# The 32-row sample tile of every projection in plain fp32, its 512 columns in four strips of 32 PSUM rows

## The chip, the cores and the metric

The kernel runs on one core of a Trainium2 chip, as one launch. Its time is the device time of one execution in microseconds (us). All rows below come from one profiled execution of it.

## The reference

The program is one inference step of a two-layer decoder for 512 prompt rows and 32 sample rows (8 sequences of 4 new tokens), all in fp32. Layer A mixes tokens with a gated MLP, layer B with differential attention over shared keys and values; after each mixer comes a mixture of 16 experts, two for each token. `x` stands for prompt and sample rows together, 544 of them.

```python
# layer A
z = gelu(x @ w_in + b_in)                # 1024 -> 2048
u, v = split(z);  v = layer_norm(v)
x = layer_norm(ALPHA * x + (u * mix(v)) @ w_out)
x = layer_norm(ALPHA * x + moe(x))       # router, top 2 of 16 experts
# layer B
k, v, q = x @ w_k, x @ w_v, x @ w_q      # 1024 -> 1024 each
x = layer_norm(ALPHA * x + heads_norm(attention(q, k, v, cache)) @ w_o)
x = layer_norm(ALPHA * x + moe(x))
```

## The kernel before

**Tiles.** The 544 rows are five tiles: four of 128 prompt rows and one of the 32 sample rows (`TILES`, `ROWS`, the sample tile is `t == TILES - 1`). A projection's weights come in blocks of 512 output columns: 4 for `w_in`, 2 for `w_out`, 6 for K, V and Q, 2 for `w_o`, so 14 blocks. A block is two chunks, for the two halves of the 1024 input rows (`kh`); a chunk is 1 MB, four groups (`j`) of 128 input rows by 512 columns.

**The split product.** Every matrix is split in two: `wh` is the chunk rounded to fp32r (ScalarE, line 617), `wl` the rest (VectorE, line 868). The input rows are transposed on TensorE (`turn`, line 1467), ScalarE rounds them into `xTh` (line 632), and VectorE takes the rest into `xTl` (line 882). A product is then three matmuls of fp32r operands (`three`, lines 1422 to 1424), with the transposed rows stationary (128 or 32 columns of them) and 512 weight columns moving. For each of 8 groups of input rows, each of the five tiles costs these three matmuls.

**Order.** `project` runs a block half by half, all five tiles in each half; `project_by_tile` runs tile after tile, both halves at once, and is used for `w_out`, the first K block and `w_o`. A tile's result lies in one of six PSUM banks (`bank_for`); VectorE evicts it (lines 934, 977 and 1267) and gives the bank back with `proj_free`. The order on each engine is the order in which the code is written. In a `w_in` block VectorE splits two chunks first and evicts then; in the third block it computes the statistics of a layer norm in between (lines 889 to 899), in the fourth it ends that layer norm (line 914).

**Buffers.** Chunks land in six `raw` slots, asked for by SyncE's queue in a written order. A slot is asked for again when VectorE has split what is in it (`low["a"]`, `low["b"]`). The split chunks lie in three slots of `wh` and `wl`, which come free with `used` when TensorE is done with a half block.

**Around the projections.** After `w_out` and after `w_o` come a layer norm, tile by tile over all engines (`ln_tiles`), and the router (`route`): TensorE transposes a tile and multiplies it with the router's weights (lines 1538 and 1541), and VectorE works out from the logits which expert gets which row. Ahead of this, `moe_act` and `moe_dve` split the first two chunks of the first expert. Attention (lines 1657 to 1760) uses plain fp32 matmuls, the sample's value product among them (line 1720, 32 stationary and 128 moving columns, once for each head):

```python
for h in range(HEADS):
    mm = pe.matmul(ps[0:NSAMP, 6 + h // 4, h % 4 * P:(h % 4 + 1) * P], ptz[:, page, b2, h],
                   vals[:, page, h * P:(h + 1) * P], ...)
```

Of the kernel before, what the change touches and what calls it, by code (L numbers as in the profile page):

```python
# [123 lines left out]
def trunk(nc, a, outs):  # L124
    y_prompt, y_sample, k_prompt, v_prompt, k_sample, v_sample, state_v = outs
    with ExitStack() as ctx:
# [19 lines left out]
        xTh = place("xTh", [P, KT_D, NTOK], F32R)[0]  # L146
        xTl = place("xTl", [P, KT_D, NTOK], F32R)[0]
# [9 lines left out]
        rwh, rwl = rwhl[:, :, 0], rwhl[:, :, 1]  # L157
        rbias = place("rbias", [P, EXPERTS], F32)[0]
# [20 lines left out]
        xT0 = place("xT0", [P, KT_D, NTOK], F32, arena)[0]  # L179
        rw_raw = place("rw_raw", [P, KT_D, EXPERTS], F32, arena + 20480)[0]  # L180
# [16 lines left out]
        mxs, n = place("mxs", [P, 4, 2, 2], F32, n)  # L197
        o = [o01[:, 0], o01[:, 1], o23[:, 0], o23[:, 1], o4[:, 0]]
# [3 lines left out]
        Es, n = place("Es", [P, 288], F32, n)  # L202
        Ps, n = place("Ps", [P, 288], F32, n)
# [3 lines left out]
        assert n <= split_at  # L207
# [85 lines left out]

        def dram_tile(t, ap):
            return ap[t * P:t * P + ROWS[t]]
# [22 lines left out]
        def _(sp):  # L318
# [50 lines left out]
            def x_half(half):  # L369

                for dst, src in ((xT0[:, 4 * half:4 * half + 4, 0:SEQ], a["x_prompt_T"]),
                                 (xT0[:, 4 * half:4 * half + 4, SEQ:NTOK], a["x_sample_T"])):
# [17 lines left out]
            def after_a(slot):  # L390
# [4 lines left out]
                else:  # L395
                    sp.wait_ge(low["a"], low_a[c])
# [9 lines left out]
            for c in range(B_CHUNKS):  # L406
# [10 lines left out]
                else:  # L417
                    sp.wait_ge(low["b"], low_b[c - RAW_SLOTS])
# [12 lines left out]
            def after_b(slot):  # L431
# [3 lines left out]
                else:  # L435
                    sp.wait_ge(low["b"], low_b[c])
# [4 lines left out]
        def _(pool):  # L441
# [19 lines left out]
            pool.dma_start(rw_raw[:], a["router_w"].rearrange("(k p) e -> p k e", p=P)).then_inc(rw_in, 16)  # L461
# [146 lines left out]
        def _(act):  # L608
# [50 lines left out]
            for half in range(2):  # L659
                act.wait_ge(xT0_in[half], 32)  # L660
                act.activation(xTh[:, 4 * half:4 * half + 4], xT0[:, 4 * half:4 * half + 4], ACT.Copy).then_inc(x0_high, 1)
                split_a(half)
            act.wait_ge(rw_in, 16)
            act.activation(rwh, rw_raw[:], ACT.Copy).then_inc(rw_high, 1)
# [191 lines left out]
        def _(dve):  # L856
# [20 lines left out]
            def turn_low(n0, gain=1.0):  # L877
                for n in (n0, n0 + 1):
                    t, half = n % 10 // 2, n % 2
                    dve.wait_ge(tr_high, n + 1)  # L880
# [926 lines left out]
```

## Time and profile before

| what | value |
|---|---|
| three timed runs | 1462.28, 1470.77 and 1472.52 us, median 1470.77 |
| span of the profiled execution, first to last instruction | 1465.0 us |
| its mean granted clock of TensorE, as a share of 2.4 GHz | 0.912 |
| TensorE matmuls, busy | 1253.8 us (86%) |
| TensorE weight loads, busy | 963.9 us (66%) |
| VectorE, busy | 916.1 us (63%) |
| ScalarE, busy | 698.6 us (48%) |
| GpSimd, busy | 252.7 us (17%) |

No time beside the span is listed for the profiled execution itself; the span is 5.8 us under the median of the timed runs. PE is TensorE, PEld its weight loads, DVE VectorE, ACT ScalarE, POOL GpSimd, SP SyncE. L1422 is line 1422 of the kernel. Busy time of matmuls counts their durations, which overlap in a pipeline; the distance from one start to the next is what one costs.

### The profile page before, as it was taken

To read this page: it belongs to the slowest core of one execution; us is meant where nothing else is said; L and a number is where in the kernel's file an instruction comes from. 1 tells how busy PE (TensorE), PEld (TensorE's weight loads), DVE (VectorE), ACT (ScalarE), POOL (GpSimd) and SP (SyncE) were. 2 spreads that over 40 slices of the span, in tenths; PEclk is the share of its full clock that TensorE was granted. 3 is DMA by queue.
4 is the path that set the end of the run, shared out by engine and by line. 5 is a ranking of instruction groups with operands and counts; after the bars stand their busy time and mean duration, and the time that the engine had idled before them with its cause. 6 is when DMAs were issued, how large, how long until landed. Compare 5 with 4: busy or idle time off the path is not lost.

```text
span 1465.0 us, 16900 instructions
## 1 busy us (share of the span) xinstructions
PE 1253.8 (86%) x5888; PEld 963.9 (66%) x5888; DVE 916.1 (63%) x1112; ACT 698.6 (48%) x748; POOL 252.7 (17%) x261
## 2 busy tenths in 40 slices
PE   5989994599999996299999999989937999999930
PEld 4766764478888885277776666657736788888820
DVE  4256357498888885832321444464675988888836
ACT  4233223277777775222112544432224777777721
POOL 2021020241111121410000000000302411112314
PEclk9999995699999998599999999969858999999975
DMA  9302047269999996732230133213462899999842
GB/s 341 122 29 93 1 173 285 84 224 359 374 372 372 376 368 214 296 116 92 89 116 1 59 116 115 78 48 118 187 238 83 302 376 373 369 375 371 299 181 77
DMA packets 142529, 302.56 MB, mean 207 GB/s; under 512 B 11888, under 2 KB 12048, under 8 KB 142352
## 3 DMA queue, kind: packets, MB, share of 16 engines
q1 hardware_dynamic: 123024, 250.23, 47.9%
q0 software_dynamic: 19168, 51.31, 9.8%
q8 instruction: 30, 0.49, 0.1%
q10 hardware_dynamic: 288, 0.36, 0.1%
q14 instruction: 19, 0.16, 0.0%
HBM read 288.36 MB, written 30.28 MB: 217 GB/s over the span
## 4 chain that ended last, share of the span: by engine, by line
PE 78%; DVE 13%; DMA 3%; ACT 3%; issue 2%; POOLq 0%; POOL 0%; SPq 0%; DVEq 0%; ACTq 0%
PE ps L1422 20%; PE ps L1424 20%; PE ps L1423 20%; PE ps L1657 3%; DVE wl L868 2%; PE ps L1720 2%; PE ps L1705 2%; PE ps L1581 2%; DVE x L1225 2%; PE ps L1467 2%; ACT wh L617 2%; PE ps L1674 1%; PE ps L1691 1%; DMA xg<-x_rows,gcur 1%; DMA yl<-y_rows 1%
## 5 line engine op out<-in xcount | busy, mean ns | idle before, releaser
L868 DVE TENSOR_TENSOR wl<-raw,wh 128x2048 fp32r<-128x2048 f32 x210 | 481.0, 2314 | 221.3 <-ACT wh L617 217.4
L617 ACT ACTIVATE wh<-raw 128x2048 fp32r<-128x2048 f32 x210 | 398.4, 1915 | 202.0 <-PE ps L1424 138.0
L1422 PE MATMUL ps<-wh,xTh 128*128 128x512 f32 (+1 forms) x560 | 227.7, 407 | 22.8 <-DVE wl L868 14.8
L1424 PE MATMUL ps<-wh,xTl 128*128 128x512 f32 (+1 forms) x560 | 223.0, 398 | 0.0
L1423 PE MATMUL ps<-wl,xTh 128*128 128x512 f32 (+1 forms) x560 | 223.0, 398 | 0.0
L1422 PE MATMUL ps<-wh,xgTh 128*128 128x512 f32 x512 | 209.3, 409 | 6.7 <-DVE xgTl L1175 5.7
L1423 PE MATMUL ps<-wl,xgTh 128*128 128x512 f32 x512 | 203.9, 398 | 0.0
L1424 PE MATMUL ps<-wh,xgTl 128*128 128x512 f32 x512 | 203.5, 398 | 0.0
L1422 PEld LDWEIGHTS ps<-wh,xTh 128*128 128x128 f32 (+1 forms) x560 | 98.6, 176 | 58.9 <-issue 22.5
L1422 PEld LDWEIGHTS ps<-wh,xgTh 128*128 128x128 f32 x512 | 97.3, 190 | 36.2 <-DVE wl L868 8.3
L1424 PEld LDWEIGHTS ps<-wh,xTl 128*128 128x128 f32 (+1 forms) x560 | 98.0, 175 | 34.2
L1423 PEld LDWEIGHTS ps<-wl,xTh 128*128 128x128 f32 (+1 forms) x560 | 98.7, 176 | 31.9
L1422 PE MATMUL ps<-wh,hTh 128*128 128x512 f32 x256 | 106.0, 414 | 9.9 <-DVE hTl L1186 9.9
L1424 PEld LDWEIGHTS ps<-wh,xgTl 128*128 128x128 f32 x512 | 97.2, 190 | 24.2
L1423 PEld LDWEIGHTS ps<-wl,xgTh 128*128 128x128 f32 x512 | 97.5, 190 | 20.5
L1424 PE MATMUL ps<-wh,hTl 128*128 128x512 f32 x256 | 103.7, 405 | 0.0
L1423 PE MATMUL ps<-wl,hTh 128*128 128x512 f32 x256 | 103.2, 403 | 0.0
L1279 DVE TENSOR_REDUCE mxs<-ps 128x1 f32<-128x256 f32 (+3 forms) x64 | 31.4, 491 | 85.8 <-PE ps L1659 85.4
L517 POOL COPY gcur<-gidx 128x1 int32 (+1 forms) x34 | 18.3, 537 | 356.6 <-PE ps L1581 295.3
L458 POOL TENSOR_TENSOR x<-x,gb 128x1024 f32<-128x1024 f32 x16 | 45.8, 2864 | 157.1 <-ACT x L648 157.1
L703 ACT ACTIVATE xgTh<-ps 128x1024 fp32r<-128x1024 f32 x34 | 34.9, 1027 | 59.9 <-PE ps L1581 59.8
L1422 PEld LDWEIGHTS ps<-wh,hTh 128*128 128x128 f32 x256 | 49.6, 194 | 21.0 <-DVE wl L868 10.4
(258 smaller groups left out, 1641.1 us busy)
## 6 DMA issues: line engine op xcount, KB each, us to landing
raw<-in_moe_w_up SPq DMA_DIRECT2D x120, 1024.0 KB, 10.5
raw<-in_moe_w_down SPq DMA_DIRECT2D x62, 1024.0 KB, 11.7
raw<-in_a_w_in SPq DMA_DIRECT2D x8, 1024.0 KB, 16.7
ahead_up<-in_moe_w_up SPq DMA_DIRECT2D x8, 1024.0 KB, 8.7
yl<-y_rows POOLq DMA_DIRECT2D x8, 1024.0 KB, 8.4
raw<-in_cache_k SPq DMA_DIRECT2D x16, 512.0 KB, 3.8
raw<-in_cache_v SPq DMA_DIRECT2D x16, 512.0 KB, 4.9
raw<-in_a_w_out SPq DMA_DIRECT2D x4, 1024.0 KB, 5.1
```

The costliest lines, as they stand in the source:

```text
L458: pool.tensor_tensor(src[0:m, t], src[0:m, t], gb[0:m, 0:D] if call else x[0:m, 0], ALU.mult).then_inc(ln_gain, 1)
L617: act.activation(wh[:, slot], src, ACT.Copy).then_inc(high[key], 1)
L703: act.activation(xgTh[:], ps[:, 2:4].rearrange("p a (k m) -> p (a k) m", m=P), ACT.Copy).then_inc(s["xg_high"], 1)
L868: dve.tensor_tensor(wl[:, slot], src, wh[:, slot].bitcast(F32), ALU.subtract).then_inc(low[key], 1)
L1225: link(dve.scalar_tensor_tensor(out=x[0:m, t], in0=yl[0:m, t, k], scalar=gates[0:m, k, t:t + 1], in1=x[0:m, t], op0=ALU.mult, op1=ALU.add))
L1279: dve.tensor_reduce(mxs[:, 1, n % 2, part:part + 1], ps[:, part, 0:w], AX, ALU.max, negate=True).then_inc(at_max, 1)
L1422: pe.matmul(out, high_, w_high, start=start, stop=False)
L1423: pe.matmul(out, high_, w_low, start=False, stop=False)
L1424: return pe.matmul(out, low_, w_high, start=False, stop=stop)
L1467: mm = pe.transpose(ps[:, 6 + n % 2, j * P:j * P + m], src[0:m, k * P:(k + 1) * P], ident[0:m, 0:m])
L1581: mm = pe.transpose(ps[:, 2 + k // 4, k % 4 * P:(k % 4 + 1) * P], xg[:, k * P:(k + 1) * P], ident)
L1657: pe.matmul(ps[:, part, 0:w], QT[r, h, qt * P:(qt + 1) * P], KT[r, h, 0:w], start=True, stop=False, skip_group_check=True)
```

## The change

The sample tile leaves the split product. Its transposed rows lie in `xs` as plain fp32, and the weights are read unsplit from the `raw` slot. For each group of 128 input rows there are four matmuls in the place of three: each has the same 32 stationary columns and 128 of the 512 moving columns, and piece `c` writes PSUM rows `32c` to `32c + 31` of the tile's bank. The 128-row tiles stay as they were. The rest follows from that: VectorE evicts the tile in four pieces; ScalarE no longer copies the sample's transposed rows, VectorE does it alone; the sample's router product is plain fp32 too; and a `raw` slot is asked for again when TensorE has used it (`used`), no longer when VectorE has split it (`low`).

```diff
+        def strip(step, c):
+            return ps[32 * c:32 * c + NSAMP, step % PROJ_BANKS, 0:P]
+        def raw_of(key, s):
+            c = s + (s >= A_WS) if key == "a" else s if s < B_CACHE else s - B_CACHE + B_WO
+            return raw[:, c % RAW_SLOTS]
...
                 if c >= RAW_SLOTS:
-                    sp.wait_ge(low["a"], low_a[c - RAW_SLOTS])
+                    sp.wait_ge(used["a"], low_a[c - RAW_SLOTS])
...
                     t, half = n % 10 // 2, n % 2
+                    if t == TILES - 1:
+                        continue
                     act.wait_ge(tr_done, n + 1)
...
+                    if t == TILES - 1:
+                        dve.wait_ge(tr_done, n + 1)
+                        dve.tensor_scalar(xs[:, 4 * half:4 * half + 4],
+                                          ps[:, 6 + n % 2].rearrange("p (k m) -> p k m", k=4)[:, :, 0:NSAMP],
+                                          gain, None, ALU.mult).then_inc(tr_low, 1)
+                        continue
...
+                if t == TILES - 1:
+                    for c in range(4):
+                        w = x[0:m, t, cb * HALF + c * P:cb * HALF + (c + 1) * P]
+                        ins = dve.scalar_tensor_tensor(out=w, in0=w, scalar=ALPHA, in1=strip(m_step, c),
+                                                       op0=ALU.mult, op1=ALU.add)
+                    ins.then_inc(proj_free, 1)
+                    return
...
+            def sample_tile(key, s, kh, step):
+                for j in range(4):
+                    k = 4 * kh + j
+                    for c in range(4):
+                        mm = pe.matmul(strip(step, c), xs[:, k], raw_of(key, s)[:, j, c * P:(c + 1) * P],
+                                       start=(k == 0), stop=(k == KT_D - 1), skip_group_check=True)
+                return mm
...
-                        for j in range(4):
+                        if t == TILES - 1:
+                            mm = sample_tile(key, s, kh, m0 + t)
+                        for j in range(4 if t < TILES - 1 else 0):
```

On TensorE, in the first half of the first block, where the fourth 128-row tile ends and the sample tile begins, there stood before (`ps` is PSUM, the shape is that of the output; the three rows of 32x512 then come three times more):

```order
L1422 MATMUL ps<-wh,xTh 128x512
L1423 MATMUL ps<-wl,xTh 128x512
L1424 MATMUL ps<-wh,xTl 128x512
L1422 MATMUL ps<-wh,xTh 32x512
L1423 MATMUL ps<-wl,xTh 32x512
L1424 MATMUL ps<-wh,xTl 32x512
```

And at the same place now:

```order
L1458 MATMUL ps<-wh,xTh 128x512
L1459 MATMUL ps<-wl,xTh 128x512
L1460 MATMUL ps<-wh,xTl 128x512
L1472 MATMUL ps<-raw,xs 32x128 x16
L1458 MATMUL ps<-wh,xTh 128x512 [waits x0_low,low_a]
```

Twelve matmuls of 512 columns have become sixteen calls of 128 columns.

On ScalarE, after `w_out`, in the layer norm and router of layer A, up to the first expert's splits and the exponential of the router, there stood before:

```order
L632 ACTIVATE xTh<-ps 128x4x128 [waits tr_done] x2
L646 ACTIVATE lns<-lns 32x1 [waits ln_var]
L648 ACTIVATE x<-x,lns 32x1024 [waits ln_rs]
L632 ACTIVATE xTh<-ps 128x4x128 [waits tr_done] x4
L632 ACTIVATE xTh<-ps 128x4x32 [waits tr_done] x2
L617 ACTIVATE wh<-raw 128x2048 [waits raw_m0_0,used_a]
L617 ACTIVATE wh<-raw 128x2048 [waits raw_m0_1,used_a]
L699 ACT_TABLE_LOAD
```

And now:

```order
L644 ACTIVATE xTh<-ps 128x4x128 [waits tr_done] x2
L658 ACTIVATE lns<-lns 32x1 [waits ln_var]
L660 ACTIVATE x<-x,lns 32x1024 [waits ln_rs]
L644 ACTIVATE xTh<-ps 128x4x128 [waits tr_done] x4
L627 ACTIVATE wh<-raw 128x2048 [waits raw_m0_0,used_a]
L627 ACTIVATE wh<-raw 128x2048 [waits raw_m0_1,used_a]
L711 ACT_TABLE_LOAD
```

The two copies of the sample tile between the last full tile and the first expert's splits are gone.

On SyncE's queue, from the `w_in` chunks after the first six to the first expert's chunks, there stood before:

```order
L386 DMA raw<-in_a_w_in 128x4x512 [waits low_a] x2
L386 DMA raw<-in_w_s_T 128x1024 [waits low_a]
L386 DMA raw<-in_a_w_out 128x4x512 [waits low_a] x4
L323 DMA raw<-in_moe_w_up 128x4x512 [waits low_a] x2
L323 DMA raw<-in_moe_w_up 128x4x512 [waits mix_done]
L323 DMA raw<-in_moe_w_up 128x4x512 [waits low_a]
L329 DMA raw<-in_moe_w_down 128x4x512 [waits low_a] x2
```

And now:

```order
L396 DMA raw<-in_a_w_in 128x4x512 [waits used_a] x2
L396 DMA raw<-in_w_s_T 128x1024 [waits used_a]
L396 DMA raw<-in_a_w_out 128x4x512 [waits used_a] x4
L333 DMA raw<-in_moe_w_up 128x4x512 [waits used_a] x2
L333 DMA raw<-in_moe_w_up 128x4x512 [waits mix_done]
L333 DMA raw<-in_moe_w_up 128x4x512 [waits used_a]
L339 DMA raw<-in_moe_w_down 128x4x512 [waits used_a] x2
```

No transfer moved; each waits for TensorE's use of the slot where it waited for VectorE's split.

## Rows read from the trace of the kernel before

**Rows 1.** The page: the chain that ended last, by engine and by line.
```profile
PE 78%; DVE 13%; DMA 3%; ACT 3%; issue 2%; POOLq 0%; POOL 0%; SPq 0%; DVEq 0%; ACTq 0%
PE ps L1422 20%; PE ps L1424 20%; PE ps L1423 20%; PE ps L1657 3%; DVE wl L868 2%; PE ps L1720 2%; PE ps L1705 2%; PE ps L1581 2%; DVE x L1225 2%; PE ps L1467 2%; ACT wh L617 2%; PE ps L1674 1%; PE ps L1691 1%; DMA xg<-x_rows,gcur 1%; DMA yl<-y_rows 1%
```

**Rows 2.** Busy time by window: length, busy by engine, granted clock, DMA share, GB/s.
```profile
310.00:560.00 250.00, 249.49 (x1152) 200.94 (x1151) 220.09 (x125) 194.96 (x136) 46.45 (x56) 1.00 0.99 358
...
680.00:740.00 60.00, 59.39 (x266) 43.89 (x266) 16.96 (x15) 10.23 (x9) 2.66 (x5) 1.00 0.32 108
```

**Rows 3.** Groups by shape: stationary rows*columns, output, count, busy us, mean ns.
```profile
L1422 PE MATMUL ps<-wh,xTh 128*32 128x512 f32 x112 | 44.3, 396 | 0.0
```

**Rows 4.** TensorE's timeline, first block: start us, duration us, line, operands.
```profile
27.68 0.39 PE L1424 MATMUL ps<-wh,xTl 128*128 128x512 f32 x1
27.90 0.39 PE L1422 MATMUL ps<-wh,xTh 128*32 128x512 f32 x1
...
30.67 0.39 PE L1422 MATMUL ps<-wh,xTh 128*128 128x512 f32 x1
```

**Rows 5.** TensorE's timeline in attention, plain fp32 operands (f32).
```profile
834.70 0.27 PE L1713 MATMUL ps<-con,Ps 128*128 128x128 f32 x1
834.81 0.27 PE L1714 MATMUL ps<-con,Ps 128*32 128x128 f32 x1
835.01 0.70 PE L1657 MATMUL ps<-KT,QT 64*128 64x256 f32 x2
...
838.73 1.93 PE L1720 MATMUL ps<-raw,ptz 128*32 128x128 f32 x16
```

**Rows 6.** TensorE's timeline in layer B's router, the sample tile.
```profile
1072.67 0.21 PE L1538 MATMUL ps<-rwhl,xTh 128*32 128x32 f32 x1
1072.73 0.20 PE L1541 MATMUL ps<-rwhl,xTl 128*32 128x16 f32 x1
```

**Rows 7.** Busy time by window, the same stretch.
```profile
1062.00:1073.30 11.30, 11.30 (x67) 11.21 (x67) 5.58 (x7) 5.41 (x7) 2.55 (x4) 0.50 0.41 127
```

**Rows 8.** Timeline of TensorE's weight loads, first block, sample tile.
```profile
27.91 0.11 PEld L1423 LDWEIGHTS ps<-wl,xTh 128*32 128x32 f32 x1
```

**Rows 9.** TensorE's timeline, layer A; in brackets: idle before, and its releaser.
```profile
109.66 0.80 PE L1422 MATMUL ps<-wh,xTh 128*128 128x512 f32 x1 [5.12 <-DVE u L977]
...
137.49 2.81 PE L1508 MATMUL ps<-v,raw 128*128 128x512 f32 x6 [0.30 <-DVE u L977]
...
212.69 1.06 PE L1467 MATMUL ps<-con,x 128*128 128x128 f32 x8 [0.41 <-PE ps L1424]
```

**Rows 10.** ScalarE's timeline in the third and fourth block of `w_in`.
```profile
87.43 1.92 ACT L617 ACTIVATE wh<-raw 128x2048 fp32r<-128x2048 f32 x1 [11.33 <-PE ps L1424]
...
123.37 1.92 ACT L617 ACTIVATE wh<-raw 128x2048 fp32r<-128x2048 f32 x1 [7.27 <-PE ps L1424]
```

**Rows 11.** VectorE's timeline after `w_out`.
```profile
214.56 0.16 DVE L898 RECIPROCAL lns<-lns 128x1 f32<-128x1 f32 x1 [4.21 <-ACT lns L646]
```

**Rows 12.** ScalarE's timeline at layer A's router.
```profile
227.71 0.60 ACT L632 ACTIVATE xTh<-ps 128x512 fp32r<-128x512 f32 x1 [0.26 <-PE ps L1467]
...
231.92 0.28 ACT L632 ACTIVATE xTh<-ps 128x128 fp32r<-128x128 f32 x1
232.09 3.70 ACT L617 ACTIVATE wh<-raw 128x2048 fp32r<-128x2048 f32 x2
```

**Rows 13.** VectorE's timeline at layer A's router.
```profile
234.02 4.49 DVE L868 TENSOR_TENSOR wl<-raw,wh 128x2048 fp32r<-128x2048 f32 x2 [1.51 <-ACT wh L617]
238.48 0.12 DVE L1026 MEMSET lg<- 128x80 f32 x1
```

**Rows 14.** The page: DMA issues, count, KB each, median us from issue to landing.
```profile
raw<-in_moe_w_up SPq DMA_DIRECT2D x120, 1024.0 KB, 10.5
```

**Rows 15.** VectorE's timeline and groups by shape: 32-row evictions in four pieces and whole.
```profile
145.62 2.15 DVE L994 SCALAR_TENSOR_TENSOR u<-ps,bss,u 32x128 f32<-32x128 f32 x8 [0.23 <-PE ps L1515]
...
216.03 0.67 DVE L934 SCALAR_TENSOR_TENSOR x<-x,ps 32x512 f32<-32x512 f32 x1
```

More of the change, by code:

```diff
@@ L145, in trunk @@
         xT_at = top[0]
-        xTh = place("xTh", [P, KT_D, NTOK], F32R)[0]
-        xTl = place("xTl", [P, KT_D, NTOK], F32R)[0]
+        xTh = place("xTh", [P, KT_D, SEQ], F32R)[0]
+        xTl = place("xTl", [P, KT_D, SEQ], F32R)[0]
         split_at = top[0]
@@ L157, in trunk @@
         rwh, rwl = rwhl[:, :, 0], rwhl[:, :, 1]
+        xs = place("xs", [P, KT_D, NSAMP], F32)[0]
+        rw32 = place("rw32", [P, KT_D, EXPERTS], F32)[0]
         rbias = place("rbias", [P, EXPERTS], F32)[0]
@@ L178, in trunk @@
         bss, n = place("bss", [NSAMP, 8], F32, n)
[L179 to L180 removed]
+        xT0 = place("xT0", [P, KT_D, SEQ], F32, arena)[0]
         QT, n = place("QT", [P, HEADS, NTOK], F32, arena)
@@ L197, in trunk @@
         mxs, n = place("mxs", [P, 4, 2, 2], F32, n)
+        Es, n = place("Es", [P, 288], F32, n)
+        Ps, n = place("Ps", [P, 288], F32, n)
         o = [o01[:, 0], o01[:, 1], o23[:, 0], o23[:, 1], o4[:, 0]]
@@ L369, in x_half @@
             def x_half(half):
-                for dst, src in ((xT0[:, 4 * half:4 * half + 4, 0:SEQ], a["x_prompt_T"]),
-                                 (xT0[:, 4 * half:4 * half + 4, SEQ:NTOK], a["x_sample_T"])):
+                for dst, src in ((xT0[:, 4 * half:4 * half + 4], a["x_prompt_T"]),
+                                 (xs[:, 4 * half:4 * half + 4], a["x_sample_T"])):
                     sp.dma_start(dst, src[half * HALF:(half + 1) * HALF].rearrange("(k p) n -> p k n", p=P)
@@ L395, in after_a @@
                 else:
-                    sp.wait_ge(low["a"], low_a[c])
+                    sp.wait_ge(used["a"], low_a[c])
             blocks = moe_stream(0, after_a)
@@ L417, in _ @@
                 else:
-                    sp.wait_ge(low["b"], low_b[c - RAW_SLOTS])
+                    sp.wait_ge(used["b"], low_b[c - RAW_SLOTS])
                 if B_CACHE <= c < B_WO:
@@ L435, in after_b @@
                 else:
-                    sp.wait_ge(low["b"], low_b[c])
+                    sp.wait_ge(used["b"], low_b[c])
             moe_stream(1, after_b)
@@ L975, in _ @@
                     dve.wait_ge(proj_done, step + 1)
+                    if t == TILES - 1:
+                        for c in range(4):
+                            c0 = WIN_COLS[j] * HALF + c * P
+                            ins = dve.tensor_tensor(dst[0:m, t, cols + c * P:cols + (c + 1) * P], strip(step, c),
+                                                    gb[0:m, c0:c0 + P], ALU.add)
+                        ins.then_inc(proj_free, 1)
+                        continue
                     bias = gb[0:m, WIN_COLS[j] * HALF:(WIN_COLS[j] + 1) * HALF]
@@ L1266, in _ @@
                     dve.wait_ge(proj_done, step + 1)
+                    if t == TILES - 1:
+                        for c in range(4):
+                            ins = dve.tensor_copy(dst[:, c * P:(c + 1) * P], strip(step, c))
+                        ins.then_inc(proj_free, 1)
+                        continue
                     dve.tensor_copy(dst, ps[0:m, step % PROJ_BANKS]).then_inc(proj_free, 1)
@@ L1487, in project_by_tile @@
                             pe.wait_ge(low[key], s + 1)
-                        for j in range(4):
+                        if t == TILES - 1:
+                            mm = sample_tile(key, s, kh, m0 + t)
+                        for j in range(4 if t < TILES - 1 else 0):
                             k = 4 * kh + j
@@ L1537, in route @@
                         for k in range(KT_D):
+                            if b == TILES - 1:
+                                mm = pe.matmul(ps[0:NSAMP, bank, b * 2 * EXPERTS:(b * 2 + 1) * EXPERTS], xs[:, k],
+                                               rw32[:, k], start=(k == 0), stop=(k == KT_D - 1), skip_group_check=True)
+                                continue
                             pe.matmul(ps[0:ROWS[b], bank, b * 2 * EXPERTS:(b + 1) * 2 * EXPERTS], xTh[:, k, tok],
```

19 lines of the change are left out of this document (9 added, 10 removed).

## The prediction

> **What bounds the kernel now.** I read the chain that ended last first: TensorE holds 78% of it [rows 1], and the three lines of the split product hold 60% of the span. Next the busy time by stage, for the stretches in which a projection runs: in the middle of the K, V and Q projections TensorE is busy for 59.39 of 60 us at the full clock while the DMA engines are a third busy [rows 2]. A microsecond of TensorE work saved there is a microsecond of the span. In the expert blocks TensorE and the DMA engines are both full [rows 2], but the change touches nothing there. Then the shapes: the 32-row tile has 112 instructions of each of the three kinds [rows 3], 336 in all; one kind stands there for the three. Their listed 393 to 396 ns are durations that overlap. The start times give the real price: twelve instructions from 27.90 to 30.67 us, 0.231 us each [rows 4]. I call three of them, 128 rows of the contraction, a step: **0.69 us now, 112 steps, 77.6 us**. That is all there is to win or lose on TensorE.
>
> **The change part by part.**
>
> *The steps.* A step becomes four calls of plain fp32 with 128 moving columns. In the trace a plain fp32 call is two instructions: the sample's value product calls 8 heads and shows 16 instructions [rows 5]. So a step is 8 instructions where there were 3. Each takes 0.11 us at the full clock (834.70 to 834.81), and with 32 stationary columns 1.93/16 = 0.12 with the ends of the run [rows 5]. The question that decides this case is whether instructions that write different strips of 32 PSUM rows run beside each other. No row of this trace shows two strips; every 32-column instruction in it writes rows 0 to 31. So both ends:
> - One after another, a step takes 8 x 0.11 = 0.88 us, 0.19 more than now.
> - Beside each other, the order of the calls still limits it. A call's two instructions write the same strip, and instructions on one strip start 0.11 apart [rows 5]. The program issues both before the next strip's first, and in every stretch that I read the matmuls start in program order. So two strips run side by side at most, and a step takes 4 x 0.11 = 0.44 us plus four times what the next strip's weight load leaves uncovered.
>
> That uncovered part is bounded by rows too. Router products with a 32-column load and hardly any columns to stream start 0.053 us apart [rows 6] at the half clock, 1.2 GHz [rows 7]; at the full clock I estimate half of it, 0.027. A load is issued when the matmul before it starts (27.91 after 27.90) [rows 4, 8]; if that also holds from strip to strip, a step takes 4 x (0.11 + 0.027) = 0.55 us. If the load of a strip that isn't in use comes earlier, 0.44. No row says which, so I take the middle, 0.50 us: **0.19 us saved a step**.
>
> The Trainium skill (TensorE: Matmul & The Clock Gate, Part 3) gives about 4 ns between matmuls on different tiles and 2.38 times the speed for three column strips; by that a step would be at the 0.44 end, and no run here shows it yet.
>
> *Where the saving counts.* Nearly everywhere TensorE goes straight on. At two places another engine sets the end. In A's third column block TensorE waits 5.12 us at 109.66 for VectorE, whose run began when ScalarE got a split buffer back at 87.43, halfway through that block [rows 9, 10]; what the second half saves only lengthens that wait. In the fourth block the run from 123.37 on ends at 137.49, with TensorE 0.30 us early already [rows 9, 10]. These two half blocks, 8 steps, gain nothing. At the end of w_out and of w_o the saving does count: VectorE sits idle 4.21 us at 214.56 for a normalise on ScalarE [rows 11], which stands behind the first transposes of the router, and these start at 212.69 [rows 9] after the sample tile. So 104 steps x 0.19 = **19.8 us off**. The ends are 104 x 0.25 = 26.0 and 104 x 0.14 = 14.6.
>
> *Entering and leaving the strips.* There are 23 stretches of strip work: 18 half blocks and 5 blocks done tile by tile. The nearest row, from 128 stationary columns to 32 and back, shows no break (27.68, 27.90, and 30.67 after the last) [rows 4]. From a 32-column product to a product over 64 rows the next start comes 0.20 instead of 0.11 later, 0.09 more [rows 5]. I take 0, and 23 x 2 x 0.09 = 4.1 us as the bad end. The Trainium skill (TensorEngine Tiling (Array Packing), Tiling Modes) says that a change of tiling mode drains the engine. The row into the 64-row product agrees, the rows at 27.68 and 27.90 don't; by its rule the sum would be 4.1 us worse.
>
> *ScalarE's copy of the tile goes.* VectorE now takes the transposed tile straight from PSUM. This counts at the router. Today ScalarE is free after 227.71 + 0.60, waits for the sample's transposes, copies them, the second half at 231.92, and only then splits the first expert's two chunks from 232.09 [rows 12]. VectorE splits after that, until 234.02 + 4.49, and starts the routing at 238.48 [rows 13]. Without the two copies ScalarE's splits fit into 228.3 to 232.1; VectorE takes the tile at 231.8, then splits for 4.49 us from about 232.2 and is ready at 236.7: 1.7 us earlier, in each layer, **3.4 us off**. TensorE's last router product, near 236.1, is then almost as late, so there is no more to have.
>
> *What that cover costs if it fails.* The raw slots are now given back when TensorE has used them, not when VectorE has split them, so SyncE's queue stands at later waits, and everything behind them in it stands too. Its first expert's chunks, all six behind slot 0's wait, can start only when w_out has ended, near 211; today they start once VectorE has split the last w_out chunk. With 10.5 us to landing [rows 14] they are there by 222, before ScalarE wants them at 228.3. Inside the projections a chunk's slot comes free more than a block before the chunk is split, and the first cache chunks' slots two blocks before attention. I cost these waits at nothing; if the first chunks came late, the 3.4 us would be lost and more.
>
> *VectorE's eviction of the tile* becomes four instructions of 128 columns: 8 such took 2.15 us, 0.27 each, so 1.08 against 0.67 [rows 15]. The 0.4 us hides in VectorE's idle time, except where VectorE is last, in A's fourth block and after w_out: 0.8 us on. The sample's router product keeps 16 short instructions; the smaller copies at the start are worth some 0.2, which I leave out.
>
> **The sum**, on the profiled span of 1465.0 us: -19.8 - 3.4 + 0.8 = -22.4 us. The three timed runs have a median of 1470.77, 5.8 above that span, and their own spread (1462.28 to 1472.52) is wider than that; I put the sum on the median: **1448 us**. With 0.44 a step it is 1442; with 0.55, the 4.1 us of breaks and no gain at the router it is 1461.
>
> **The rivals.**
> - *The strips don't run beside each other* (slower). The place is every step, the price 0.19 us. Only the four steps before the 5.12 us stall are covered, so 108 x 0.19 = 20.5, less the 2.6 of the other parts: **1489 us**; by 0.12 an instruction, 1497. It decides as soon as a step costs more than 0.71. For it: no row shows an overlap, and this is the plain reading of rows 5. Against it: the four calls write different rows and need nothing of each other. It is also the case in which the change doesn't do what it says.
> - *The next strip's load is not covered* and costs the whole 0.053 of rows 6: 4 x 0.163 = 0.65 us a step, 104 x 0.04 = 4.2 off, with the other parts 6.8: **1464 us**. For it: loads are issued one ahead, no more [rows 8]. Against it: those rows are at the half clock. The Trainium skill (the same Part 3) has loads overlap running matmuls only when their row groups differ, and here all strips use the same rows; that would favour this rival, but the load at 27.91 runs beside a matmul on the same rows, so the trace disagrees.
> - *All four strips side by side*, the two instructions of a call no longer in each other's way: 0.22 a step, 104 x 0.47 = 48.9, with the rest 51.5 off: **1419 us**. Against it: starts in program order.
>
> **How the numbers follow.** Forecast 0.60, one after another 0.20, load uncovered 0.13, all four 0.06. The range leaves out the last and slivers: 1440 to 1491. Within the forecast alone it is 1442 to 1461. A measurement of this kernel tells about 1% from no change, 14.7 us. Faster by more than that, below 1456: nine tenths of the forecast and the all-four case, 0.60. Slower, above 1485: most of the first rival, 0.18. Between: 0.22.
>
> **What would show it.** In the changed profile, the start of a strip's first instruction after its neighbour's second: 0.005 to 0.03 us if I am right, 0.05 in the second rival, 0.11 in the first. A half tile of four steps should take 1.8 to 2.2 us, where 2.77 stood. TensorE's wait at 109.66 should grow by about what a half block saves, and the routing should start about 1.7 us earlier after the last sample transposes. I am wrong if strip starts are 0.11 apart throughout, or if ScalarE waits there for a DMA of the first expert.

## The result, and the profile after

The changed kernel takes **1416.92 us** (median of 5 runs, 1414.52 to 1425.42), the kernel before 1472.12 (5 runs, 1462.28 to 1473.16): a ratio of 0.9645, 95% interval 0.9616 to 0.9673, or 55 us less. In a second set it had a median of 1423.75 (6 runs, 1412.58 to 1424.34) against 1472.43, ratio 0.9658 (0.9625 to 0.9691). The forecast of 1448 us was wrong, and the range (1440 to 1491) left the time out. The last rival, all four strips side by side at 1419 us, is what happened. The profiled execution of the changed kernel is the slowest of its five: span 1423.6 us, time 1425.42.

The page, the chain that ended last, by engine (answers to [rows 1]):

```profile
PE 70%; DVE 14%; DMA 9%; ACT 4%; issue 2%; POOLq 0%; SPq 0%; POOL 0%; DVEq 0%; ACTq 0%
```

TensorE's timeline in the first block, the half tile that [rows 4] show (start us, duration us, line, operands, count):

```profile
28.13 0.39 PE L1460 MATMUL ps<-wh,xTl 128*128 128x512 f32 x1
28.45 1.08 PE L1472 MATMUL ps<-raw,xs 128*32 128x128 f32 x32
29.46 0.50 PE L1458 MATMUL ps<-wh,xTh 128*128 128x512 f32 x1
29.80 0.40 PE L1459 MATMUL ps<-wl,xTh 128*128 128x512 f32 x1
```

All 32 instructions of a half tile lie within 1.08 us, where the forecast had 1.8 to 2.2. The reader can also see three distances between starts that are wider than usual: 0.32 before the strips (usual: 0.23), 0.20 from the last strip instruction's start (29.26) to 29.46 (usual behind an instruction of 128 columns: 0.11), and 0.34 from 29.46 to 29.80 (usual: 0.23). From the start of the product ahead (28.13) to 29.80 there are 1.67 us; less two usual distances (0.46) and four steps (8 x 0.109 = 0.87), that leaves 0.33 us for entering and leaving. Before, the same stretch took 3.22 (0.23 + 12 x 0.23 + 0.23). **A half tile saves 1.55 us.** Summed over the 23 stretches of the two traces (28 half tiles), the saving is 47.8 us.

The group of the strip products (count, then min/median/max in ns):

```profile
L1472 PE MATMUL ps<-raw,xs x896: 272/273/298, 28.5 to 1004.3; 128*32 128x128 f32 x180
```

All 112 steps are there, 8 instructions each. Without any break 28 half tiles would have saved 28 x (2.77 - 0.87), some 53 us; the traces show 47.8, so entering and leaving took some 5 us in all. The 0.33 us are the price in the six stretches that other products of the same block follow. In most of the others it is about 0.17, because the kernel before had a longer distance at that place too, mostly 0.69 to 0.70 us from a block's last product to the next block's first (usual: 0.23), where there are 0.61 now (usual: 0.11).

Where in the span the time went, by the start of the first instruction of each stage:

| stage begins with | before | changed | gained in the stage ahead |
|---|---|---|---|
| first mix product (end of `w_in`) | 137.49 | 125.52 | 12.0 |
| first transpose for `w_out` | 147.82 | 137.18 | -1.3 |
| router A, first transpose | 212.69 | 194.07 | 8.0 |
| routing A, VectorE | 238.48 | 218.41 | 1.5 |
| attention, first product | 799.35 | 756.23 | 23.0 |
| first transpose for `w_o` | 985.54 | 947.23 | **-4.8** |
| router B, first transpose | 1050.11 | 1005.04 | 6.8 |
| routing B | 1075.91 | 1029.38 | 1.5 |
| end of the span | 1465.04 | 1423.57 | **-5.1** |

Without the two bold lines these add up to some 51.4 us. The bold lines are work that the change doesn't touch. Layer B's gather holds most of the second: its products began 26.8 us after the routing in the profile of before, and 30.5 to 30.9 us after it in the changed kernel and in every experiment. In layer A they began 30.7 us after it in the profile of before too, so the 26.8 is the odd one; with one profile of that kernel, why stays open. The first is attention; the runs below show that it follows the granted clock.

Rows of TensorE that answer to [rows 9] (in brackets: idle before, and its releaser):

```profile
101.04 0.80 PE L1458 MATMUL ps<-wh,xTh 128*128 128x512 f32 x1 [6.98 <-DVE u L1009]
...
125.52 7.11 PE L1557 MATMUL ps<-v,raw 128*128 128x512 f32 x16 [0.74 <-DVE wsm L994]
...
137.18 1.97 PE L1514 MATMUL ps<-con,u 128*128 128x128 f32 x8 [2.70 <-DVE u L1026]
...
194.07 1.06 PE L1514 MATMUL ps<-con,x 128*128 128x128 f32 x8 [0.44 <-PE ps L1472]
```

The wait in the third block has grown from 5.12 to 6.98, by about one half tile's saving. At 125.52 and at 137.18 it is VectorE that TensorE waits for. The second of these waits was half as long in the kernel before:

```profile
147.82 1.20 PE L1467 MATMUL ps<-con,u 128*128 128x128 f32 x8 [1.37 <-DVE u L994]
```

ScalarE's timeline at layer A's router (answers to [rows 12]):

```profile
209.55 0.60 ACT L644 ACTIVATE xTh<-ps 128x512 fp32r<-128x512 f32 x1 [0.26 <-PE ps L1514]
210.04 3.70 ACT L627 ACTIVATE wh<-raw 128x2048 fp32r<-128x2048 f32 x2
```

And VectorE's, up to the start of the routing (answers to [rows 13]):

```profile
213.33 0.72 DVE L894 TENSOR_SCALAR xs<-ps 128x128 f32<-128x128 f32 x2 [2.45 <-PE ps L1514]
213.96 4.48 DVE L880 TENSOR_TENSOR wl<-raw,wh 128x2048 fp32r<-128x2048 f32 x2
218.41 0.12 DVE L1058 MEMSET lg<- 128x80 f32 x1
```

ScalarE's splits of the first expert follow straight on the last 128-row copy, and no DMA holds them up. VectorE takes the sample tile, splits, and starts the routing 24.3 us after the router's first transpose, where it was 25.8.

### The profile page after: what moved, and what is told of

The parts are those of the page before. It is cut to its first block, busy times and chain, and to the rows that moved or that the text cites. A ratio compares the mean times of both kernels' runs of the same rounds, so it can differ in the third digit from the quotient of the medians.

```text
span 1423.6 us, 18050 instructions
## 1 busy us (share of the span) xinstructions
PE 1206.3 (85%) x6448; PEld 953.2 (67%) x6448; DVE 922.0 (65%) x1152; ACT 695.5 (49%) x738; POOL 264.4 (19%) x261
## 4 chain that ended last, share of the span: by engine, by line
PE 70%; DVE 14%; DMA 9%; ACT 4%; issue 2%; POOLq 0%; SPq 0%; POOL 0%; DVEq 0%; ACTq 0%
PE ps L1458 17%; PE ps L1460 17%; PE ps L1459 17%; DMA raw<-in_moe_w_down 6%; DVE wl L880 3%; PE ps L1710 3%; ACT wh L627 3%; PE ps L1773 2%; PE ps L1758 2%; PE ps L1514 2%; PE ps L1634 2%; PE ps L1472 2%; DVE x L1256 2%; PE ps L1727 1%; DMA xg<-x_rows,gcur 1%
## 5 line engine op out<-in xcount | busy, mean ns | idle before, releaser
L1458 PE MATMUL ps<-wh,xTh 128*128 128x512 f32 x448 | 183.6, 410 | 25.4 <-DVE wl L880 15.2
L1459 PE MATMUL ps<-wl,xTh 128*128 128x512 f32 x448 | 178.2, 398 | 0.0
L1460 PE MATMUL ps<-wh,xTl 128*128 128x512 f32 x448 | 178.2, 398 | 0.0
L1458 PEld LDWEIGHTS ps<-wh,xTh 128*128 128x128 f32 x448 | 86.8, 194 | 47.3 <-issue 21.5
L1460 PEld LDWEIGHTS ps<-wh,xTl 128*128 128x128 f32 x448 | 86.3, 193 | 19.0
L1459 PEld LDWEIGHTS ps<-wl,xTh 128*128 128x128 f32 x448 | 87.0, 194 | 16.9
L527 POOL COPY gcur<-gidx 128x1 int32 (+1 forms) x34 | 22.0, 647 | 356.2 <-PE ps L1634 298.8
L537 POOL DMA_INDIRECT y_rows<-yb,scur x32 | 36.9, 1153 | 147.1 <-ACT yb L732 121.7
```

The lines of the kernel that those rows point to most:

```text
L537: pool.indirect_dma_start(y_rows[l], bass.IndirectOffsetOnAxis(ap=scur[:, 0:1], axis=0), yb[:], None, bounds_check=2 * NTOK - 1, oob_is_er ...
L1458: pe.matmul(out, high_, w_high, start=start, stop=False)
L1459: pe.matmul(out, high_, w_low, start=False, stop=False)
L1460: return pe.matmul(out, low_, w_high, start=False, stop=stop)
```

## The experiments

The question is what let four strips run at once when starts were expected in program order. The theory after the result: TensorE keeps the strips apart and passes over an instruction whose strip is busy. The rivals: program order with neighbours only, or a gain that doesn't come from the strips.

**1. Strip after strip** (a line for each strip, so that the trace names it).

```diff
-                for j in range(4):
-                    k = 4 * kh + j
-                    for c in range(4):
-                        mm = pe.matmul(strip(step, c), xs[:, k], ...
+                for j in range(4):
+                    k = 4 * kh + j
+                    mm = pe.matmul(strip(step, 0), xs[:, k], ...
+                for j in range(4):
+                    k = 4 * kh + j
+                    mm = pe.matmul(strip(step, 1), xs[:, k], ...
...
```

> The changed kernel with the two loops of the sample tile exchanged: all four steps of the first strip, then all four of the second, and so on, each strip's call on a line of its own, so that the trace tells the strips apart. Same instructions, same work. Theory: TensorE keeps the strips apart by itself and starts an instruction as soon as its own strip is free, whatever stands ahead of it for another strip; then a half tile still takes about 1.10 us, the four lines start 0.007 us apart, and the time stays within 5 us of the changed kernel's 1417. Rival (the order rule of the prediction): starts follow the program, and only neighbours on different strips run beside each other; then the eight instructions of a strip run 0.109 us apart before the next strip begins, a half tile takes 32 x 0.109 + 0.2 = 3.7 us, 2.6 more, times 26 half tiles that count: about 1484.

Measured: 1454.21 us (6 runs, 1445.13 to 1458.16), ratio 0.9892 (0.985 to 0.9934). That is neither the theory's 1417 nor the rival's 1484. TensorE's timeline; L1472, L1475, L1478 and L1481 are the strips 0 to 3:

```profile
27.27 0.73 PE L1472 MATMUL ps<-raw,xs 128*32 128x128 f32 x5
27.73 0.30 PE L1475 MATMUL ps<-raw,xs 128*32 128x128 f32 x1
27.84 0.27 PE L1472 MATMUL ps<-raw,xs 128*32 128x128 f32 x1
27.87 0.27 PE L1475 MATMUL ps<-raw,xs 128*32 128x128 f32 x1
27.95 0.27 PE L1472 MATMUL ps<-raw,xs 128*32 128x128 f32 x1
27.98 0.27 PE L1475 MATMUL ps<-raw,xs 128*32 128x128 f32 x1
28.05 0.27 PE L1472 MATMUL ps<-raw,xs 128*32 128x128 f32 x1
28.08 0.38 PE L1475 MATMUL ps<-raw,xs 128*32 128x128 f32 x2
28.20 0.30 PE L1478 MATMUL ps<-raw,xs 128*32 128x128 f32 x1
```

Strip 1 starts together with the fifth of strip 0's eight instructions, ahead of three that stand before it in the program. So starts do **not** follow the program. But TensorE doesn't pass over everything either: the next strip comes 0.47 us behind, each time when three of the row are left. A half tile's starts spread over 2.19 us instead of 0.81. Over the 23 stretches that is 35.8 us more than in the changed kernel; the medians differ by 37 (30 from the second set's).

**2. One strip.**

```diff
-            return ps[32 * c:32 * c + NSAMP, step % PROJ_BANKS, 0:P]
+            return ps[0:NSAMP, step % PROJ_BANKS, c * P:(c + 1) * P]
```

> The changed kernel with all four pieces in the first strip: the same 16 calls a half tile with the same operands, written to rows 0 to 31 at columns 0, 128, 256 and 384 of the bank, evicted in four pieces as now. Theory (the strips are the gain): the 32 instructions of a half tile run one after another 0.109 us apart, 3.49 us where the strips take 1.10, 2.4 more times 26 that count, less some 0.1 each for breaks that go: 1417 + 60 = about 1477, slower than the kernel before. Rival (the gain comes from plain fp32 out of the unsplit weights and from the shorter way to the router, not from the strips): within 5 us of 1417.

Measured: 1486.6 us (4 runs, 1484.4 to 1494.36), ratio 1.0116 (1.0066 to 1.0165). (Four sums are open at once in the same rows of a bank, and part of the sample tile's sums is missing from its results; instructions and operands are the same, so the time can be compared.) TensorE's timeline:

```profile
27.00 0.39 PE L1460 MATMUL ps<-wh,xTl 128*128 128x512 f32 x1
27.32 3.68 PE L1472 MATMUL ps<-raw,xs 128*32 128x128 f32 x32
30.93 0.50 PE L1458 MATMUL ps<-wh,xTh 128*128 128x512 f32 x1
31.27 0.40 PE L1459 MATMUL ps<-wl,xTh 128*128 128x512 f32 x1
```

The strips are the gain; plain fp32 without them is 1.2% slower than the kernel before. The time is some 10 us above the 1477 expected: by the traces the 23 stretches take 72.0 us more than in the changed kernel, where 60 were expected. This is the prediction's first rival as it would have looked (1489 us). The breaks of 0.32 and 0.34 us are here too, so they don't come from strips side by side.

**3. Two strips of 256 columns** (two calls a step, two pieces in each eviction).

```diff
-            return ps[32 * c:32 * c + NSAMP, step % PROJ_BANKS, 0:P]
+            return ps[32 * c:32 * c + NSAMP, step % PROJ_BANKS, 0:2 * P]
...
-                    for c in range(4):
-                        mm = pe.matmul(strip(step, c), xs[:, k], raw_of(key, s)[:, j, c * P:(c + 1) * P],
+                    for c in range(2):
+                        mm = pe.matmul(strip(step, c), xs[:, k], raw_of(key, s)[:, j, 2 * c * P:2 * (c + 1) * P],
```

> The changed kernel with two strips of 256 columns in place of four of 128: two calls a step on strips 0 and 1, evicted in two pieces. Theory (a strip takes as long as its own columns, and strips don't disturb each other): 8 rounds of 256 columns at about 0.216 us are 1.73 us a half tile with 0.23 for entry and exit, 1.96, 0.86 more times 26: 1417 + 22 = about 1439. Rival (TensorE takes a certain number of columns in a time, however they lie on strips, or the rounds are bound by the loads): 1417 in the second case, since half as many loads are made, and in the first too, since the columns are the same.

Measured: 1438.88 us (4 runs, 1437.98 to 1439.34), ratio 0.9772 (0.9732 to 0.9812). TensorE's timeline:

```profile
28.64 1.92 PE L1472 MATMUL ps<-raw,xs 128*32 128x256 f32 x16
```

As expected: 0.22 us an instruction of 256 columns, two side by side, and 22.9 us more over the 23 stretches than in the changed kernel. (That the median meets 1439 to the microsecond is partly luck: the changed kernel's own two medians lie 7 us apart.) This is what the forecast's 0.44 us a step would have taken.

**4. Four stretches** of one step each, behind each of the 128-row tiles, in the 18 half blocks.

```diff
+                        if kh == 0:
+                            bank_for(m0 + TILES - 1)
+                        mm = sample_tile(key, s, kh, m0 + TILES - 1, range(t, t + 1))
```

> The changed kernel with the sample tile's half block cut into four stretches of one step, one behind each of the 128-row tiles, in the 18 half blocks of the projections that go by half block; the work is the same. Theory: entering and leaving the strips costs 0.23 us a stretch (0.09 at the entry, 0.02 in the first round, 0.11 at the exit), so 54 more stretches are 12.4 us, less what falls before waits: about 1428, and each single step shows 0.45 us between its neighbours. Rival (the break is one of the first and last matmul's own pipeline and is hidden when short): within 4 us of 1417.

Measured: 1439.57 us (4 runs, 1436.7 to 1448.06), ratio 0.9798 (0.9746 to 0.985), 22.7 us above the changed kernel. TensorE's timeline around one step:

```profile
18.89 0.39 PE L1460 MATMUL ps<-wh,xTl 128*128 128x512 f32 x1
19.21 0.43 PE L1472 MATMUL ps<-raw,xs 128*32 128x128 f32 x8
19.56 0.50 PE L1458 MATMUL ps<-wh,xTh 128*128 128x512 f32 x1
19.90 0.39 PE L1459 MATMUL ps<-wl,xTh 128*128 128x512 f32 x1
```

From 18.89 to 19.90 are 1.01 us, less two usual distances (0.46) and the step itself (0.22): **0.33 us a stretch**. I had left out the late product behind the first one (19.56 to 19.90). 54 x 0.33 = 18 us, against 22.7 by the medians (15.8 from the second set's). The trace shows a new wait besides, ahead of one step:

```profile
635.36 0.42 PE L1472 MATMUL ps<-raw,xs 128*32 128x128 f32 x8 [2.61 <-DVE stg L1303]
```

**5. ScalarE's copy back**, and a line for each strip in the changed kernel's own order.

```diff
-                    if t == TILES - 1:
-                        continue
                     act.wait_ge(tr_done, n + 1)
+                    if t == TILES - 1:
+                        act.activation(xs[:, 4 * half:4 * half + 4], ..., ACT.Copy, scale=gain).then_inc(tr_high, 1)
+                        continue
...
```

> The changed kernel with ScalarE copying the transposed sample tile out of PSUM again, as before the change (VectorE only passes the news on), and with each strip's call on a line of its own, in the same order as in the changed kernel. Two questions. First the router: by the prediction's term the copies hold up ScalarE's splits of the first expert, so the routing should start 1.5 us later after the router's first transpose than in the changed kernel (25.8 us after it instead of 24.3), in both layers; the rival says the 1.5 us came from the shorter router product of the tile, and then it stays at 24.3. Second the order: by the theory that TensorE passes over instructions that wait for their strip, the four lines start 0.007 us apart, then the same four again 0.109 us later, though the program holds both instructions of a call next to each other; the rival says that each call's two instructions follow each other before the next line's first, which the step of 0.22 us would have to come from in another way.

Measured: one run, 1426.56 us, span 1424.7. The routing starts 26.26 us after the router's first transpose in both layers, 1.9 later than in the changed kernel and 0.5 later than in the kernel before; what the 0.5 are wasn't looked into. VectorE's split now waits for ScalarE (VectorE's timeline):

```profile
213.64 4.50 DVE L883 TENSOR_TENSOR wl<-raw,wh 128x2048 fp32r<-128x2048 f32 x2 [4.99 <-ACT wh L627]
218.10 0.12 DVE L1060 MEMSET lg<- 128x80 f32 x1
```

And the order (TensorE's timeline; L1474 to L1477 are the strips 0 to 3):

```profile
27.43 0.27 PE L1474 MATMUL ps<-raw,xs 128*32 128x128 f32 x1
27.43 0.27 PE L1475 MATMUL ps<-raw,xs 128*32 128x128 f32 x1
27.44 0.27 PE L1476 MATMUL ps<-raw,xs 128*32 128x128 f32 x1
27.45 0.27 PE L1477 MATMUL ps<-raw,xs 128*32 128x128 f32 x1
27.54 0.27 PE L1474 MATMUL ps<-raw,xs 128*32 128x128 f32 x1
```

The four strips start within 0.02 us of each other, and again 0.11 us later. A call's two instructions follow each other on their strip at 0.11 us, and the other strips' come in between. That the two stand next to each other in the program is taken, no run shows it; in runs 1, 6 and 9 whole calls are overtaken, so those don't need it.

**6. Pairs**: two steps of a strip in a row, then the next strip.

```diff
-                for j in range(4):
-                    k = 4 * kh + j
-                    for c in range(4):
-                        mm = pe.matmul(strip(step, c), ...
+                for jj in range(0, 4, 2):
+                    for j in (jj, jj + 1):
+                        k = 4 * kh + j
+                        mm = pe.matmul(strip(step, 0), ...
...
```

> The changed kernel with the sample tile's calls in another order: two steps of the first strip, the same two of the second, third and fourth, then the other two steps. Same work, the trace tells the strips apart. Theory from the run strip by strip: TensorE passes over waiting instructions, but over no more than three matmuls and their loads; with four instructions of a strip in a row the second strip then starts at once, the third when the first has started its second, the fourth one later, a half tile's starts spread over 1.04 to 1.15 us instead of 0.81, and the time is 1417 + 27 x 0.23 to 0.34 = about 1424. Rival one (it passes over everything): 0.81 and 1417. Rival two (it passes over one strip's run of waiting instructions only, so that strips go two by two): 1.75 in all, 1417 + 23 = 1440.

Measured: 1420.56 us (4 runs, 1419.98 to 1423.05), ratio 0.966 (0.9628 to 0.9693). TensorE's timeline; L1473, L1476, L1479 and L1482 are the strips:

```profile
27.43 0.30 PE L1473 MATMUL ps<-raw,xs 128*32 128x128 f32 x1
27.44 0.30 PE L1476 MATMUL ps<-raw,xs 128*32 128x128 f32 x1
27.45 0.30 PE L1479 MATMUL ps<-raw,xs 128*32 128x128 f32 x1
27.47 0.30 PE L1482 MATMUL ps<-raw,xs 128*32 128x128 f32 x1
27.56 0.27 PE L1473 MATMUL ps<-raw,xs 128*32 128x128 f32 x1
```

My theory fell: strip 3 starts at once, ahead of nine matmuls of the other three strips that still wait, and a half tile's starts spread over 0.85 us. So TensorE isn't limited to passing over three in all; a limit above nine isn't excluded. A limit for each strip fits: three waiting behind the one that has started, and then the row's next instruction blocks what stands behind it. That explains this run (four in a row: one started, three waiting) and the first (the fifth must start before the eighth has a place).

**7. Joined**: both half tiles of a block in one stretch.

```diff
-                        if t == TILES - 1:
-                            mm = sample_tile(key, s, kh, m0 + t)
+                        if t == TILES - 1 and kh == 1:
+                            sample_tile(key, s0, 0, m0 + t)
+                            mm = sample_tile(key, s, 1, m0 + t)
...
-                    sp.wait_ge(used["a"], low_a[c - RAW_SLOTS])
+                    sp.wait_ge(used["a"], whole(low_a[c - RAW_SLOTS]))
```

(`whole` rounds the count up to the end of the block, for all four such waits of SyncE.)

> The changed kernel with both half tiles of a block done in one stretch, at the end of the block, in the nine blocks that go by half block; a raw slot is then given back at the end of its block in both halves. Theory (a stretch costs 0.33 us: 0.09 at the entry, 0.02 in its first round, 0.11 at the exit and 0.11 at the first product after it): nine stretches fewer, of which one stands before a wait, are 2.7 us: about 1414. Rival: the later release of the first half's slot brings the chunks two blocks on later, and the time rises above 1417.

Measured: 1416.68 us (5 runs, 1414.88 to 1419.83), ratio 0.9624 (0.9597 to 0.9651); the changed kernel in the same set 0.9658 (0.9625 to 0.9691). The intervals overlap, so the times don't tell the two apart. In the trace the end of `w_in` comes 3.5 us earlier than in the changed kernel, of which 1.2 are there already ahead of the first strip, and from the first K block's sample tile to attention it takes 1.1 us less. That is 3.4 us at the strips, near the 2.7 expected. A raw slot that is given back later still shows no cost.

**8. The changed kernel again.**

> The changed kernel itself once more, to be compared with the joined stretches on the same chip and to see how its profiled span varies. Theory (the 4.8 us that attention took longer in its profile came from the clock that this execution was granted, not from the change): 1417 within 4 us, attention between 182 and 191 us, and the stretches outside it as before within 1 us. Rival (the change slows attention): 190 us or more there again.

Measured: 1423.75 us (6 runs, 1412.58 to 1424.34), above the 4 us that I had given it, and attention took 190.9 us again, which lies in the theory's bounds and in the rival's; the other stages are as before within 1 us. What decides is the busy time by window over attention (length, then busy by engine, then granted clock, DMA share, GB/s). The kernel before:

```profile
799.40:985.50 186.10, 174.84 (x972) 119.45 (x972) 91.35 (x261) 83.72 (x237) 4.44 (x6) 0.94 0.23 80
```

The changed kernel, in its first profile:

```profile
756.20:947.20 191.00, 179.75 (x972) 123.06 (x972) 90.85 (x261) 84.07 (x237) 4.48 (x6) 0.92 0.23 80
```

The kernel with four stretches:

```profile
778.10:961.00 182.90, 171.16 (x973) 117.70 (x973) 91.30 (x262) 83.58 (x237) 4.48 (x6) 0.97 0.24 84
```

The joined kernel:

```profile
751.00:944.20 193.20, 183.06 (x973) 124.80 (x973) 91.44 (x261) 84.14 (x237) 4.47 (x6) 0.89 0.25 85
```

The instructions are the same; the length goes with the clock, 182.9 us at 0.97, 186.1 at 0.94, 191.0 at 0.92, 193.2 at 0.89. By these means some 11, 22, 31 and 43 us ran at the half clock (an estimate: twice the missing share, times the length), and 10 us of that cost about 3. The run strip by strip has 182.8 at 0.97. All but the first contain the change to attention's surroundings, and they lie on both sides of it. So the 4.8 us were the clock. But the changed kernel's own two profiles got 0.92 both times, and so did run 5, which has the same order of calls (191.0 us). Whether the change brings this lower clock about stays open.

**9. Threes**: three steps of a strip in a row, then the fourth of each.

```diff
-                for j in range(4):
-                    k = 4 * kh + j
-                    for c in range(4):
-                        mm = pe.matmul(strip(step, c), ...
+                for js in ((0, 1, 2), (3,)):
+                    for j in js:
+                        k = 4 * kh + j
+                        mm = pe.matmul(strip(step, 0), ...
...
```

> The changed kernel with three steps of a strip in a row for each strip in turn, then the fourth step of each; same work, a line for each strip. The run strip by strip (eight instructions in a row) and the one in pairs (four in a row) together suggest that each strip has a queue of its own that takes the started instruction and three more, and that TensorE goes on to the next strip as soon as the last of a row has a place in it. Theory: with six in a row the next strip starts together with the third of the six, 0.24 us behind the strip before it; four strips lie 3 x 0.24 us apart and the last runs 0.79 us, so a half tile's starts spread over 1.51 us, and a profiled span is 27 x 0.7 = 19 us longer than the changed kernel's 1422. Rival one (a strip's row is passed over whatever its length up to six): 0.85 as in pairs. Rival two (a row longer than four holds the next strip up to its end, as if in program order): the next strip starts with the sixth, 0.57 us later, and the spread is 2.5 us.

Measured: one run, 1439.62 us, span 1437.8. TensorE's timeline; L1473, L1476 and L1479 are the strips 0 to 2:

```profile
27.53 0.52 PE L1473 MATMUL ps<-raw,xs 128*32 128x128 f32 x3
27.78 0.30 PE L1476 MATMUL ps<-raw,xs 128*32 128x128 f32 x1
...
28.03 0.30 PE L1479 MATMUL ps<-raw,xs 128*32 128x128 f32 x1
```

Strip 1 comes with the third of strip 0, 0.25 us behind its first, strip 2 another 0.25 behind; the starts of a half tile spread over 1.53 us (expected: 1.51). This is the forecast of the limit for each strip, and both rivals fall. The span is 14 to 15 us longer than the changed kernel's, not 19. One part of that is the blocks done tile by tile, where the second half tile begins while the first still runs: 1.03 us lost for two half tiles there, 0.7 for one elsewhere, 17.4 us over all stretches. Another is the third block of `w_in`, where TensorE's wait falls from 6.98 to 6.26 us.

## Why the prediction was wrong

**The bound** was read rightly: what TensorE saved at the strips (47.8 us) is almost all in the time, 55 us by the first set's medians and 49 by the second's.

**The steps: here it failed.** The sentence is "The program issues both before the next strip's first, and in every stretch that I read the matmuls start in program order. So two strips run side by side at most". The second half doesn't follow: no row there shows two strips, so they can't show what happens between strips. Runs 1, 6 and 9 show that TensorE lets a strip's instruction start ahead of earlier ones of another strip, and they fit a limit of three waiting in each strip. (That the built program keeps the written order of the calls is taken; a trace shows starts alone.) A step costs 0.22 us and not 0.50. Run 3 shows that the 0.44 of the forecast is what two strips would have cost. The last rival had the right step; I gave it 0.06 on the strength of the same inference, and cut it out of the range. That its 1419 us came out so close is partly luck: it left the breaks out, and by measured terms its 51.5 us off would have been 47.5 (the sum below).

The Trainium skill (TensorE: Matmul & The Clock Gate, Part 3) says of matmuls on different tiles that they begin and end in program order, and that only weight loads are pulled ahead. Run 1 disagrees: line L1472 has starts at 27.84, 27.95 and 28.05, after L1475's first at 27.73, though all of L1472 stands first. The prediction also quotes from there 2.38 times the speed for three strips and puts that at its 0.44 end. This was misread: two strips side by side give twice the speed at most (run 3), so the figure spoke for the last rival.

**The load** of the next strip: bounded at 0 to 0.053 us, measured as nothing; the strips' first instructions start 0.007 us apart.

**Entering and leaving**: taken at 0, with 4.1 us as the bad end; it took some 5 us, 0.33 us a stretch between products of one block and about 0.17 in most others. Rows 4 misled: the 32-column product there is fp32r. The trace of before held a nearer row, from 128 to 32 columns with both in plain fp32:

```profile
843.60 0.63 PE L1691 MATMUL ps<-con,raw 128*128 128x128 f32 x4
844.15 1.93 PE L1720 MATMUL ps<-raw,ptz 128*32 128x128 f32 x16
```

The last of the four starts at 843.95 (0.63 less one duration of 0.28 behind 843.60), so the next one comes 0.20 us behind it where 0.11 is usual: the 0.09 of the entry. Eleven such runs in attention show it; a lone product of 32 columns (834.81 in [rows 5]) doesn't, and why not stays open. Run 2 has the break with plain fp32 on the first strip alone. The Trainium skill's rule (TensorEngine Tiling (Array Packing), Tiling Modes) that a change of mode drains the engine fits the 32-column runs in plain fp32, the changed kernel's and run 2's; the fp32r run in rows 4 shows no such drain.

**Where the saving counts**: the third block's second half is lost as said (5.12 to 6.98 us of wait). In the fourth block both halves counted at first (109.66 to 137.49 was 27.83 us, 101.04 to 125.52 is 24.48), and 1.3 us were given back behind the mix products, where TensorE's wait for VectorE has grown from 1.37 to 2.70. So of the two half blocks that were to gain nothing there, the fourth block's did gain a part. VectorE's longer evictions (term: 0.8 in all) may show here. How the 1.3 us divide between the evictions and VectorE's masking, which now stands last before the mix, wasn't tried.

**The router**: 1.7 us a layer forecast, 1.5 measured, and 1.9 when the copy goes back (run 5). Right, by the mechanism named.

**The raw slots** cost nothing, as taken: no wait for a DMA at 210.04, and none from holding them longer still (run 7).

**The sum** by measured terms: stretches 47.8, less the wait's growth of 1.9 and the 1.3 behind the mix, plus 2.9 at the router, is 47.5 us; the stages that the change touches gained 51.4 by the two profiles, and the medians differ by 55. The last 4 to 8 us aren't explained; the two medians of the changed kernel (1416.92 and 1423.75) differ by as much.

## What to carry to other kernels

A small-M product in plain fp32 can be cut by columns into four strips of PSUM rows and runs four times as fast as on one strip (0.22 us a step against 0.87, run 2), if the calls go round the strips so that no strip has more than four instructions (two fp32 calls) in a row. Keep strip work together: a stretch between products of another kind cost 0.33 us, and 54 more of them some 18 us (run 4); nine fewer were too few to show in the time (run 7). Where no row of a trace shows two things that could run side by side, "in order" read from rows in which they couldn't is no evidence: leave the full overlap inside the range. Before explaining a few microseconds in a stage that a change doesn't touch, lay its length beside its granted clock.

## What the runs showed of the hardware

- TensorE starts matmuls out of the written order between strips. Three runs fit a limit for each strip, one started instruction and three waiting, so that the fifth in a row blocks what stands behind it. Delay of the next strip behind the one before: 0.01 us with four in a row (run 6), 0.25 with six (run 9), 0.47 with eight (run 1).
- Strips don't slow each other: 0.109 us an instruction of 128 columns with one strip in use (run 2, 32 in 3.49 us) and with four.
- A run of plain fp32 products with 32 stationary columns between fp32r products of one block with 128 costs 0.33 us (28.13 to 29.80): 0.09 at the entry, 0.02 in the first round, 0.11 at the exit and 0.11 between the first and the second product behind it.
